# A state-space stage rewritten: the next group's convolution beside this group's chunk steps

## What is computed

```python
def ssm_prep(u, p):
    ...
    xbc = jax.nn.silu(dw_conv_centred(xbc, p['ssm_conv_w'], p['ssm_conv_b']))   # five taps
    ...
    dt = jax.nn.softplus((dt.reshape(b_, n, 2, SSM_HEADS) + p['ssm_dt_bias']).astype(F32))
...
    def step(h, inp):
        x_c, dt_c, b_c, c_c = inp
        cum = jnp.cumsum(dt_c * ag, axis=1)
        xdt = x_c * dt_c[..., None]
        h_new = h * jnp.exp(cum[:, -1])[..., None, None] + jnp.einsum('bjgn,bjge,bjgep->bgepn', b_c, jnp.exp(cum[:, -1:] - cum), xdt)
        if not with_output:
            return h_new, None
        seg = jnp.exp(jnp.where(lower, cum[:, :, None] - cum[:, None, :], -jnp.inf))
        cb = jnp.einsum('bign,bjgn->bijg', c_c, b_c)
        y_intra = jnp.einsum('bijg,bijge,bjgep->bigep', cb, seg, xdt)
        y_inter = jnp.einsum('bign,bgepn->bigep', c_c, h) * jnp.exp(cum)[..., None]
        return h_new, y_intra + y_inter
```

## Time and profile before

| | us |
|---|---|
| median of 3 runs | 5768.94 |
| lowest and highest | 5765.70, 5770.66 |
| the profiled execution | 5778.16 |
| its span, first to last instruction | 5776.5 |
| mean granted clock of TensorE | 0.882 of 2.4 GHz |

### The profile page before, as it was taken

One profiled execution on the slowest core, in us unless ns is written; L12 is line 12 of the kernel. 1 busy time (PEld: TensorE's weight loads), 2 busy tenths in 40 slices (PEclk: granted clock), 3 DMA queues, 4 the chain that ended last, 5 costly groups with the idle time before them and its releaser, 6 DMA issues. The chain is left out here.

```text
span 5776.5 us, 90470 instructions
## 1 busy us (share of the span) xinstructions
PE 4594.3 (80%) x38042; PEld 3533.5 (61%) x38042; DVE 2785.3 (48%) x4473; ACT 1562.2 (27%) x2461; POOL 462.8 (8%) x471
## 2 busy tenths in 40 slices
PE   6999688888874444695687867767999999787999
PEld 4888567777763333573222345444788878676787
DVE  4556566666656666553000034545444322276553
ACT  3222232222322222232000032323322221364332
POOL 0000110100002222200000001211000000000000
PEclk8999899999986676797799977777999999899999
DMA  6656600000000000321999631001122223311332
GB/s 225 227 190 233 216 10 16 13 20 13 6 29 20 31 31 15 123 90 45 381 422 422 268 116 40 15 30 64 53 64 66 70 74 115 119 42 60 96 98 95
DMA packets 168388, 616.29 MB, mean 107 GB/s; under 512 B 24224, under 2 KB 37536, under 8 KB 142688
## 3 DMA queue, kind: packets, MB, share of 16 engines
q1 hardware_dynamic: 153072, 544.03, 26.3%
q0 software_dynamic: 14960, 67.12, 2.9%
HBM read 533.32 MB, written 77.75 MB: 106 GB/s over the span
## 5 line engine op out<-in xcount | busy, mean ns | idle before, releaser
L1666 PE MATMUL f_acc<-f_a_lo,f_w_hi 128*128 128x512 f32 x4048 | 1029.5, 357 | 67.5 <-DVE f_a_lo L1888 30.5
L1666 PEld LDWEIGHTS f_acc<-f_a_lo,f_w_hi 128*128 128x128 f32 x4048 | 666.6, 190 | 190.3 <-issue 44.5
L1666 PE MATMUL f_acc<-f_a_lo,f_w_lo 128*128 128x512 f32 x2288 | 685.6, 355 | 0.0
L1655 DVE TENSOR_TENSOR f_w_lo<-f_w_raw,f_w_hi 128x1024 fp32r<-128x1024 f32 (+1 forms) x176 | 228.4, 1298 | 539.6 <-ACT f_w_hi L1650 539.6
L1666 PEld LDWEIGHTS f_acc<-f_a_lo,f_w_lo 128*128 128x128 f32 x2288 | 378.5, 190 | 64.3
L1650 ACT CAST f_w_hi<-f_w_raw 128x1024 fp32r<-128x1024 f32 (+1 forms) x176 | 195.2, 1109 | 612.6 <-DMA f_w_raw<-in_ffn_w_up 217.6
L335 DVE COPY_PREDICATED rw_work<-rw_mask_x,rw_big 128x512 f32<-128x512 uint8 x288 | 238.7, 882 | 159.3 <-PE rw_big L626 154.2
L1666 PE MATMUL i_acc<-i_x_hi,i_w_hi 128*128 128x512 f32 (+1 forms) x1024 | 306.8, 355 | 10.4 <-DVE i_x_lo L2421 10.0
L1666 PE MATMUL i_acc<-i_x_lo,i_w_hi 128*128 128x512 f32 (+1 forms) x1024 | 305.6, 354 | 0.0
L1666 PE MATMUL i_acc<-i_x_hi,i_w_lo 128*128 128x512 f32 (+1 forms) x1024 | 305.3, 354 | 0.0
L1310 PE MATMUL ex_big<-ex_w,ex_xe_now 128*64 128x512 f32 x1024 | 240.8, 625 | 77.5 <-DMA ex_w<-in_exp_w 77.5
(11 more groups left out here) (514 smaller groups left out, 8453.9 us busy)
## 6 DMA issues: line engine op xcount, KB each, us to landing
ex_w<-in_exp_w SPq DMA_DIRECT2D x192, 1024.0 KB, 17.4
i_mod_rows<-in_ada_rows SPq DMA_DIRECT2D x128, 512.0 KB, 4.7
f_w_raw<-in_ffn_w_up SPq DMA_DIRECT2D x88, 512.0 KB, 3.5
i_w_raw<-in_w_in_both SPq DMA_DIRECT2D x44, 512.0 KB, 3.6
f_w_raw<-in_ffn_w_down SPq DMA_DIRECT2D x32, 704.0 KB, 4.1
i_w_raw<-in_w_in_lat SPq DMA_DIRECT2D x40, 512.0 KB, 4.4
pt<-i_stage POOLq DMA_DIRECT2D x22, 768.0 KB, 5.5
f_w_raw<-in_hgrn_w_both SPq DMA_DIRECT2D x24, 512.0 KB, 3.5
```

Source lines behind the costliest of these rows:

```text
L1655: dve.tensor_tensor(self.view(self.w_lo, u), self.view(self.w_raw, u), self.view(self.w_hi, u).bitcast(F32), ALU.subtract).then_inc(self.r ...
L1666: op = pe.matmul(acc[:, a:b], part[:, k], xs[:, k0 + k, a:b], start=(first and k == 0 and part is w_hi and xs is x_hi), stop=(last and k = ...
```

## The change

The groups are written out instead of a loop over them, and both directions alternate: step s is (n, direction), so that `steps` goes over n first. There are 12 steps in a group, s from 0 to 11; the outputs begin at s = 4.

- During the steps of group g, DVE and ACT work on the convolution of group g+1. ACT copies the tiles and does the first tap (s = 1 to 3), DVE does the other four taps (from s = 2 on, two of 128x770 in each step, four at s = 2 and 3), ACT's sigmoids stand at s = 8 and after the steps, and TensorE and ACT turn the new x during s = 10 and 11 and after the steps (`turn`, `turned`; nine of them with the product of C and B among them). `xtok`, `btok` and the B and C tiles have two buffers. All turns use one bank.
- The mask is added on TensorE. A matmul of the identity with a tile of 0 and -1e30, both fp32r, opens the bank of `cum_rows`, and the four matmuls of the sums add to it. ACT takes the exponential straight from PSUM with the negated own sum as bias, in four instructions of 128x128 for each half. DVE's subtraction is gone, and `cbm` is a plain copy (`cbt`).
- The four output chunks stay in PSUM banks 0 to 3 through both directions. TensorE puts d times x into them (products `xs` by POOL, a matmul with the identity each), the intra matmuls add to them, and so does a matmul with the identity of `tmp`, the state's part. DVE's two additions in each step are gone. ACT copies the four finished chunks to `ys`.
- After the turn of `ys` DVE multiplies straight from PSUM. z of group g+1 is fetched when the output of group g is computed, all weights of the taps at the start, x of group g+2 when the convolution of g+1 is done. SP stores the output in place of POOL.
- The rows for the half-steps of the next step are issued during this one; `seg` has four buffers, `h` has two for each direction.

```diff
+        ident_r, mask_r = sb("ident_r", [P, CH], F32R), sb("mask_r", [P, 2, 4, CH], F32R)
...
+        xtok, btok, cbt = sb("xtok", [P, 2, 6 * 512]), sb("btok", [P, 2, 6, CH]), sb("cbt", [P, 2, 4, CH])
+        xw, xdt, xs = sb("xw", [P, 2, 512]), sb("xdt", [P, 2, 512]), sb("xs", [P, 2, 512])
+        seg = sb("seg", [P, 4, 4, CH])
+        h, hf, tmp = sb("h", [P, 2, 2, 512]), sb("hf", [P, 512]), sb("tmp", [P, 2, 512])
...
+        ROWS_B, INTER, STATE, TR = (4, 5), 6, 7, 7
...
+        steps = [(n, d) for n in range(6) for d in range(2)]
...
+                def load_group(g):
+                    if g >= 1:
+                        sp.wait_ge(S["permuted"], 3 * g)
+                        sp.wait_ge(S["conv_done"], 3 * g)
+                    for a, n, first in ((0, 4, g * 4 + XBC_T), (4, 1, g + XBC_T + 16), (5, 1, g + XBC_T + 20)):
+                        sp.dma_start(nat[:, a:a + n, :], pt[first:first + n, :, 0:LAT].rearrange("a p t -> p a t")).then_inc(S["group_in"], 16)
...
+                load_group(0)
+                load_z(0)
+                load_group(1)
+                for g in range(NG):
+                    if g + 2 < NG:
+                        load_group(g + 2)
+                    sp.wait_ge(S["out_done"], g + 1)
+                    sp.dma_start(u_out[g * 4:g * 4 + 4].rearrange("a p t -> p a t"), ez[:]).then_inc(S["stored"], 16)
+                    if g + 1 < NG:
+                        load_z(g + 1)
...
+                def conv_tap(g, pair, k):
+                    if k == 1:
+                        dve.wait_ge(S["tap_done"], 3 * g + pair + 1)
+                    dve.drain()
+                    for t in (2 * pair, 2 * pair + 1):
+                        last = dve.scalar_tensor_tensor(tile(g, t), raw[:, t, k:k + CV_OUT], par[:, 6 * g + t, k:k + 1], tile(g, t), ALU.mult, ALU.add)
+                    if k == CONV - 1:
+                        last.then_inc(S["conv_done"], 1)
...
+                def silu(g, pair):
+                    dve.wait_ge(S["sig_done"], 3 * g + pair + 1)
+                    dve.tensor_tensor(tiles(g, pair), tiles(g, pair), ex_tiles(pair), ALU.mult).then_inc(S["silu_done"], 1)
...
-                            dve.tensor_scalar(xbc[:, t, :], raw[:, t, 0:CV_OUT], par[:, t, 0:1], par[:, t, 5:6], ALU.mult, ALU.add)
-                        for k in range(1, CONV):
-                            dve.drain()
-                            for t in tiles:
-                                dve.scalar_tensor_tensor(xbc[:, t, :], raw[:, t, k:k + CV_OUT], par[:, t, k:k + 1], xbc[:, t, :], ALU.mult, ALU.add)
-                        dve.drain().then_inc(S["conv_done"], 1)
...
+                for g in range(NG):
+                    more = g + 1 < NG
+                    for s, (n, d) in enumerate(steps):
...
+                            if n:
+                                dve.drain()
+                                dve.tensor_tensor(heads(hf[:]), heads(h[:, d, n % 2]), kind(ETOT, c, d, g), ALU.mult)
+                                dve.drain()
+                            dve.wait_ge(S["state_ready"], state_no(g, n, d) + 1)
+                            if n:
+                                dve.tensor_tensor(h[:, d, (n + 1) % 2], hf[:], big[:, STATE, :], ALU.add).then_inc(S["h_done"], 1)
+                            else:
+                                dve.tensor_copy(h[:, d, (n + 1) % 2], big[:, STATE, :]).then_inc(S["h_done"], 1)
...
-                            dve.tensor_tensor(ys[:, c], ys[:, c], tmp[:], ALU.add)
-                            dve.drain()
-                            dve.wait_ge(S["intra_ready"], g * 16 + (2 * m + 2))
-                            dve.tensor_tensor(ys[:, c], ys[:, c], big[:, intra_bank, :], ALU.add)
-                            dve.drain().then_inc(S["y_done"], 1)
...
+                            m = out_no(g, n, d)
+                            dve.wait_ge(S["inter_ready"], m + 1)
+                            if m >= 2:
+                                dve.wait_ge(S["tmp_used"], m - 1)
+                            dve.tensor_tensor(heads(tmp[:, m % 2]), heads(big[:, INTER, :]), kind(ECUM, c, d, g), ALU.mult).then_inc(S["tmp_done"], 1)
...
+                        if more:
+                            if s == 2:
+                                conv_tap(g + 1, 0, 1)
+                                conv_tap(g + 1, 0, 2)
+                            if s == 3:
+                                conv_tap(g + 1, 0, 3)
+                                conv_tap(g + 1, 0, 4)
+                            if 4 <= s < 8:
+                                conv_tap(g + 1, 1, s - 3)
+                            if s >= 8:
+                                conv_tap(g + 1, 2, s - 7)
+                            if s in (8, 9):
+                                silu(g + 1, s - 8)
+                    if more:
+                        dve.drain()
+                        silu(g + 1, 2)
...
                     for t in range(4):
-                        dve.tensor_tensor(ez[:, t].rearrange("p (r c) -> p r c", c=GRID), yf[:, t].rearrange("p (c r) -> p r c", r=ROWS),
...
+                        dve.wait_ge(S["ty_ready"], 4 * g + t + 1)
+                        last = dve.tensor_tensor(ez[:, t].rearrange("p (r c) -> p r c", c=GRID), big[:, t, :].rearrange("p (c r) -> p r c", r=ROWS),
...
+                def permute(g, pair):
+                    act.wait_ge(S["group_in"], 96 * g + 96)
+                    for t in (2 * pair, 2 * pair + 1):
+                        last = act.copy(raw[:, t, 2:LAT + 2].rearrange("p (c r) -> p c r", r=ROWS), nat[:, t].rearrange("p (r c) -> p c r", c=GRID))
+                    last.then_inc(S["permuted"], 1)
+                    act.drain()
+                    for t in (2 * pair, 2 * pair + 1):
+                        last = act.activation(tile(g, t), raw[:, t, 0:CV_OUT], ACT.Identity, scale=par[:, 6 * g + t, 0:1], bias=par[:, 6 * g + t, 5:6])
...
+
+                def gate(g, pair):
+                    act.wait_ge(S["conv_done"], 3 * g + pair + 1)
+                    if pair == 2:
+                        act.wait_ge(S["silu_done"], 3 * g + 1)
...
+
+                def turned(g, k):
+                    act.wait_ge(S["tr_ready"], TURNS * g + k + 1)
+                    if k < 6:
...
+                def y_copy(g, k):
+                    c = (2, 1, 3, 0)[k]
+                    act.wait_ge(S["tmp_used"], 8 * g + 4 + k + 1)
+                    act.copy(ys[:, c], big[:, c, :]).then_inc(S["ys_copied"], 1)
...
+                for pair in range(3):
+                    permute(0, pair)
...
+                    more = g + 1 < NG
+                    for s, (n, d) in enumerate(steps):
+                        c = ORDER[d][n]
+                        if more and 1 <= s <= 3:
+                            permute(g + 1, s - 1)
+                        if more and s == 8:
+                            gate(g + 1, 0)
+                            gate(g + 1, 1)
...
+                            for half in range(2):
+                                b = 2 * m + half
+                                if b >= 4:
+                                    act.wait_ge(S["intra_ready"], b - 3)
+                                act.wait_ge(S["row_ready"], b + 1)
+                                for e in range(4):
+                                    k = GH * g + 4 * half + e
+                                    last = act.activation(seg[:, b % 4, e], big[:, ROWS_B[half], CH * e:CH * e + CH], ACT.Exp, bias=kinds[:, NCUM, c, d, k:k + 1])
+                                last.then_inc(S["exp_done"], 1)
+                                if more and s >= 10:
+                                    turned(g + 1, 3 * (s - 10) + half)
+                            if more and s >= 10:
+                                turned(g + 1, 3 * (s - 10) + 2)
+                        if s == 11:
+                            y_copy(g, 0)
+                            y_copy(g, 1)
+                    if more:
+                        gate(g + 1, 2)
+                    act.wait_ge(S["z_in"], 16 * g + 16)
+                    if g:
+                        act.wait_ge(S["stored"], 16 * g)
+                    act.activation(ez[:], z[:], ACT.Sigmoid).then_inc(S["z_sig"], 1)
+                    y_copy(g, 2)
+                    y_copy(g, 3)
+                    if more:
+                        for k in range(6, TURNS):
+                            turned(g + 1, k)
...
+                            i = state_no(g, n, d)
+                            if i >= 2:
+                                pool.wait_ge(S["state_ready"], i - 1)
+                            pool.tensor_tensor(heads(xw[:, i % 2]), tok(c), kind(WJ, c, d, g), ALU.mult).then_inc(S["xw_done"], 1)
+                        if s < 4:
+                            if 4 * g + s >= 2:
+                                pool.wait_ge(S["skip_done"], 4 * g + s - 1)
```

(58 more changed lines are left out.)

327 lines of the change are left out of this document (111 added, 216 removed).

## The result

The changed kernel takes 5533.49 us in the median of 4 runs (5524.20 to 5546.16), the one before 5769.80 in 4 runs beside it (5765.70 to 5777.16). The ratio is 0.9584, 95% interval 0.9559 to 0.9609: faster by 236 us. I had forecast 5580 and 5535 as the lower end of the range. Repeated later with five runs it took 5532.71, ratio 0.9571 (0.9551 to 0.9591).

A forecast was written before the change was run, and what follows sets the result against it. No engine was full in a group; a chain through DVE, ACT, POOL and TensorE held each step. The stage's end, 1790 + 3 x 90 + 80 + 3 x 15 + 10 = 2195 against 2384.9, gave 5580 us, range 5535 to 5645.

The forecast's parts named there:

- better than 5545: Whole kernel: a time under 5545 us, from the lower bound's terms; chance 0.09.
- first group: Steps of a group with convolution beside them: 84 us, with 6 for clock and stray waits 90.
- last group: Steps of the group that has no convolution beside it: 80 us.
- three gaps: Boundaries from the last tmp matmul to the next state matmul: copies, sigmoid, product, turns and transposes, 15 us each.
- I take 8.0 us a step: Middle step: DVE and POOL take turns for 7.4 us, plus some 0.1 for each of six handovers.
- lower bound: Stage with 6.9 us a step, a head of 17, a boundary of 12 and no stray waits: 5500 us.
- clock and stray waits: Allowance added to each group's 84 us: 6 us, making 90.
- head: Steps 0 to 3 of a group, state matmuls and DVE additions alternating at half clock, then taps and products: 20 us.
- slower: Steps: rows held back by exp_done, work in sequence, 18.1 us a step, 5899 us; chance 0.04.
- DVE sets the pace: Steps: each tap and hf waits for a whole POOL product, 8.1 us a step, 5610 us; chance 0.22.
- Clock low: TensorE in the steps: low clock in part, 5630 to 5700 us, chance 0.08; throughout, 5751 and above, 0.03.
- No overlap: Convolution: x late, permutation and taps slip behind the steps, 34 us return for three groups, 5680 us; chance 0.04.

The follow-up runs named there:

- e13: Changed kernel with a piece added behind the last group, timing DVE taps or additions and POOL products alone and together; one execution of 5645.22 us.
- e1: Changed kernel with the mask matmul issued twice in every set of rows; 5550.06 us, ratio 0.9627.
- e2: Changed kernel with the mask matmul left out and the own sum without its sign as bias; 5532.52 us, ratio 0.9585.
- e4: Changed kernel with ACT's two sigmoids of step 8 issued behind that step's exponentials; 5528.73 us, ratio 0.9583.
- e10: Changed kernel with sigmoids moved, output transposes mixed with the last turns, and a group's first two sets of rows issued with its first two state matmuls; 5503.77 us.
- e5: Changed kernel with the subtraction back on DVE, one 128x512 exponential from SBUF and no mask matmul; 5579.11 us, ratio 0.9668.
- e6: Changed kernel with both additions into ys back on DVE, without tmp and skip matmuls and ACT's copies to ys; 5540.11 us, ratio 0.9604.
- e9: Changed kernel with the rows issued one half-step ahead in place of two; 5535.36 us, ratio 0.9583.
- e3: Changed kernel with DVE's taps for the next group, the sigmoids and all nine turns put after the steps; 5582.84 us, ratio 0.9676.

## Why the prediction missed its range

The direction held, and the order of the work came out as described, but not what sets the pace of a step. The range's low end was 5535 us, the median 5533.5. What came was the case "better than 5545", which had 0.09. The stage was forecast at 477.5 us (1717.5 to 2195) and took 424.2. By its own terms:

| term | forecast | measured |
|---|---|---|
| until the first state matmul | 72.5 | 72.6 |
| first group | 90 | 83.7 |
| second, third group | 90, 90 | 78.5, 78.6 |
| last group | 80 | 64.1 |
| three gaps | 15 each | 13.6 to 13.7 |
| end | 10 | 5.7 |

The start was right to 0.1 us in sum, as errors cancelled (taps from 28.1 us after the stage's begin, forecast 29; turns of 1.79, forecast 1.65). The gaps were right to 1.3.

**The failed step is "I take 8.0 us a step",** with the 7.4 us of turns and the 0.1 for each of six handovers. Measured were 6.6. I had read the lock of the earlier trace rows as excluding whole instructions; e13 shows that each pair overlaps by 0.32 us, so that the turns come to about 6.4 without handovers, and e1 and e2 show that TensorE's sum then sets the pace. My full-clock sum of 6.9 us, the lower bound, was nearer: it had 0.96 for a 512-column matmul (0.86), and 0.23 for the mask by the earlier trace rows, which e1 and e2 confirm (0.24 and 0.23).

**A second term failed with it,** and by size it is the larger one: the 6 us a group for "clock and stray waits". In middle steps the granted clock is 1.00, that is 2.4 GHz, and no stray wait appears. The lower clock is where TensorE waits, in the first group's head (0.68), at step 8 (0.76) and in the gap (0.63), and the head and the gap were costed with rows at half clock already. For them it was counted twice. In the later heads even that was too much: the second group's first two rounds of state matmul and addition take 1.90 and 1.97 us at a granted clock of 1.00, not the 2.8 of half clock, and its third addition ends 5.7 us after the head's start, not 8.4.

Of the 11.5 us that the second group was shorter than forecast, 6 are this allowance, 4.2 are steps 5 to 7 (19.8 against 24) and 3.9 the head (16.1 against 20); step 4 took 0.4 more, step 8 0.6 more and the last three steps 1.6 more. Step 8 hides a second error: its stall is 5.0 to 7.8 us by e4, not 3, because ACT idles 2.6 us for the last tap between its two sigmoids. The last group, 15.9 us shorter than forecast, has the fast steps, no allowance and a head of 13.4.

Two sums don't come out as written, though the forecast doesn't hang on them. The lower bound's group of 70 us is 17 + 6 x 6.9 + 7.5 + 5.5 + 3 = 74.4 by its own terms, and the end of "slower" is 1790 + 4 x 166 + 63 = 2517, not 2515.

**The signs.** Exponentials: 4 in 1.14 us, 2.3 a step, forecast 2.2. Taps in the steps: 1.38 us in the mean; the forecast's 1.3 to 1.9 was for the median, which is 1.51 for the x tiles and 1.02 for the B and C tiles. TensorE busy in the steps: 100% of three steps; 79% at a clock of 0.91 over two groups with their gaps. No wait of a group for its x or z appears once the steps have begun.

**The rivals.** "DVE sets the pace" (5610): not in the middle steps, where DVE is busy 96% but TensorE 100%. It holds in e10's head, by a little in e2's first group, and in the steps once DVE has some 2 us more to do, as e5 and e6 show. The Trainium skill's SBUF — State Buffer, section "SBUF: two separate sides", has the two engines lock each other out for the whole instruction; e13 measures 23.6 us where that gives 27.5 and the side by side 15.8, so the lock is real and is 0.32 us a pair shorter. "Clock low": refuted in the steps. "Slower" by rows held back: e9, with the rows one half-step later, prices that at 1.1 us a step. "No overlap" (100 us): e3 prices it at 57, since what leaves the steps shortens them.

## What to carry to other kernels

Work put beside other work costs what it adds to the fullest engine, not its own sum: 33 us of convolution in the gap cost 12.6 in the steps, 5 of them by ACT's order, and the 2.3 us of subtraction cost 2.0 a step, though TensorE had lost the mask's 0.5, because DVE was at 96%. Take the clock term for the pieces in which TensorE waits and not again as an allowance. Look at the order on the engine that serves two chains: three lines of ACT's order and the order of the last turns gave 24 to 30 us of stage after a rewrite had given 243.

## What was not expected of the hardware

- DVE with both inputs in SBUF and POOL exclude each other except for 0.32 us in each pair, the same for operations of 0.69 and of 1.02 us; with one DVE input in PSUM there is no cost (15.9 against 15.8 us).
- An fp32r mask matmul of 512 columns costs 0.23 to 0.24 us of TensorE at the full clock in this stage, while its record lasts 0.48.
- A float32 matmul of 512 columns in two passes costs 0.86 us at the full clock, while its two records together last 1.02.
- The same instructions, step 4 of a group, ran at a granted clock of 1.00 in one execution and of 0.83 in another, 8.4 against 10.0 us.
